# Combining the last three expert tiles on chip instead of two, in a mixture-of-experts kernel

## The chip, the cores and the metric

One core of a Trainium2 chip runs the whole program. The metric is the time of one execution on the device, in microseconds (us). Engines are named as in the profile: PE is TensorE, DVE VectorE, ACT ScalarE, POOL GpSimd, SP SyncE.

## The reference

One transformer-like block over 512 tokens of width 1024, in float32: a gated mixer, then a mixture of experts, then a final norm. Only the end matters here:

```python
x = x + g_f * grouped_moe(hf, ...)      # every token goes to 2 of 16 experts
return rmsnorm(x, final_norm_g)
# grouped_moe, per token t and expert e, combine[t, e] the weight of its two experts, else 0:
g = jnp.einsum('td,edf->tef', t, w_gate)
u = jnp.einsum('td,edf->tef', t, w_up)
a = jax.nn.silu(g) * u * combine[:, :, None]
y = jnp.einsum('tef,efd->td', a, w_down)     # d = 1024, f = 512
```

## The kernel before

The tokens of each expert are gathered into tiles of up to 128 rows. There are 16 tiles and as many more as experts have over 128 tokens; with these inputs the number `tiles` is 17. Each float32 product is made of three passes of `fp32r` on TensorE: a matrix is split into `hi` (a rounded copy, made by ScalarE) and `lo` (the rest, a subtraction on VectorE, L747, that reads both from SBUF), and L1321 to L1323 are hi·hi, hi·lo, lo·hi. Raw weights land in six slots of `raw`, their splits lie in six slots of `wsplit`.

Per tile i, TensorE does `gate_up`, the index of tile i + 2 and the turn of the gathered rows of tile i + 1, then `down` of tile i − 1, and turns the hidden tile (`turn_hidden`, L1575) for the next `down`. VectorE makes one-hot selections, six `lo` splits, `hidden` (L1209: silu(gate) · up), `a_lo` (L1213, the low part of the turned hidden tile `aT`) and `results` (L1227), which scales the tile's output into `y` in SBUF. GpSimd gathers the rows of a tile from DRAM (L461) and scatters `y` into a table of pairs in DRAM (L469): each token has two rows there, one for each expert. Rows that don't belong to a tile have a destination past the table's end and aren't written.

The end of the program, the tail, is written out by hand on every engine:

- The last two tiles are not scattered. Their scaled outputs stay on chip, split into `y_hi`/`y_lo`, and TensorE adds them to the right tokens by one-hot matrices `tail_sel` (L1267; product L1607 in `tail_add(j, t, part, ...)`, j the tile, t the part of 128 tokens, two halves of 512 columns each, into the PSUM pair of t). With 2 tiles, 4 parts, hi and lo and 2 halves there are 32 such products.
- The next-to-last tile's output lies in PSUM banks 5 and 6 (scaling L1277, ScalarE's `y_hi` L714, `y_lo` L1280), the last one's in banks 2 and 3 (L1292, L717, L1298).
- SyncE loads the final norm's gain row (L406), waits for the last scatter (`scattered`) and for all slots of `raw` to be free (`lo_ready`), then reads the table back as four blocks of 1 MB (L410), one for each part of 128 tokens, into slots 2 to 5 of `raw`.
- GpSimd adds the two rows of each pair (L503, one 128x1024 sum for each part, behind `y_in[t]`), VectorE adds that sum to `x_tiles` (L1285, `pair_added(t)`), and later the PSUM pair (L1307). ScalarE squares (L721), VectorE takes the root (L758 to L770) and scales parts 2 and 3 (L1313), GpSimd and ScalarE parts 0 and 1 (L510, L726), and four DMAs write the output.

All buffers are placed by hand, all waits are semaphores with counts; the order on an engine is the order in which its instructions are written.

The two lines that hold SyncE in the tail are

```python
wait_reg(sp, scattered, tiles * 16 - 32)      # 15 scatters of 16 counts each
wait_reg(sp, lo_ready, tiles * 6 + 30)        # all six slots of raw have been split
```

Of the kernel before, what the change touches and what calls it, by code (L numbers as in the profile page):

```python
# [11 lines left out]
ds = bass.ds  # L12
# [30 lines left out]
TILES_MAX = E + 8  # L43
LAST_BANK = 2
SKIP = 2048


def tokens_moe_kernel(nc, A, out):
# [18 lines left out]
    with ctx:  # L67
        def sb(name, shape, dt=F32):
            return ctx.enter_context(nc.sbuf_tensor(name, shape, dt))
# [44 lines left out]
        aT = sb("aT", [P, 2, NF, P], F32R)  # L114
        with nc.sbuf_tensor("below_tail", [P, 3 * D], F32), nc.sbuf_tensor("tail_sel", [P, 2, SEQ], F32R) as tail_sel:
            pass
# [23 lines left out]
        rt = work[:, 3 * D + NT * P:5 * D]  # L140
        gfin = work[:, 4 * D:5 * D]
        y_hi = [wsplit[:, 2 + j, 0, 0:D] for j in range(2)]
        y_lo = [wsplit[:, 2 + j, 1, 0:D] for j in range(2)]
        pair = [ps[:, 0:2, :], ps[:, 4:6, :], ps[:, 6:8, :], ps[:, 2:4, :]]
# [128 lines left out]
        def _(sp):  # L273
# [128 lines left out]
            for c in range(2):  # L402
                wait_reg(sp, lo_ready, tiles * 6 + (25 + c))
                load(c, w_down[ds(e, 1), :, 2 * c:2 * c + 2, :].rearrange("a p k f -> (a p) k f"), 2)

            sp.dma_start(gfin, A["final_norm_g"].partition_broadcast(P)).then_inc(gfin_in, 16)  # L406
            wait_reg(sp, scattered, tiles * 16 - 32)
            wait_reg(sp, lo_ready, tiles * 6 + 30)
            for t in range(NT):
                sp.dma_start(raw[:, t + 2, :], y_pairs[t]).then_inc(y_in[t], 16)  # L410
            for t in range(2, NT):
# [6 lines left out]
        def _(pool):  # L418
# [75 lines left out]
            tiles = pool.value_load(expert_of[0:1, 31:32], min_val=0, max_val=7) + E  # L494
            with pool.Fori(2, tiles - 1) as i:
                gather(i + 2)
                scatter(i - 1)
            wait_reg(pool, gathered, tiles * 16 + 16)
            wait_reg(pool, scattered, tiles * 16 - 32)

# [13 lines left out]
        def _(act):  # L514
# [190 lines left out]
            for c in range(2):  # L705
                act.wait_ge(landed[c], tiles * 16 + 14 * 16)
                act.wait_ge(chunk_used, tiles * 6 + (25 + c))
                A_(wsplit[:, c, 0, :], raw[:, c, :], ACT.Copy).then_inc(hi_ready, 1)
            act.wait_ge(chunk_used, tiles * 6 + 30)
            a_hi(tiles - 1)  # L710

            act.wait_ge(y_ready, tiles - 1)
            act.wait_ge(chunk_used, tiles * 6 + 28)
            A_(y_hi[0].rearrange("p (b n) -> p b n", b=2), ps[:, 5:7, :], ACT.Copy).then_inc(tail_hi, 1)  # L714
            for half in range(2):
                act.wait_ge(y_ready, tiles + half)
                A_(y_hi[1][:, half * 512:half * 512 + 512], ps[:, LAST_BANK + half, :], ACT.Copy).then_inc(tail_hi, 1)  # L717

# [14 lines left out]
        def _(dve):  # L733
# [524 lines left out]
            with dve.Fori(2, tiles - 1) as i:  # L1258
                tile(i, expert_ahead(i), i * 6 + 34, True, i * 6 + 36)
            step(V.tensor_scalar(tail_idx[:, :], row_dest[:, ds(tiles - 2, 2)], 1, None, ALU.logical_shift_right))  # L1260
            done()
            step(V.tensor_copy(tail_tok[:, :], tail_idx[:, :]))
            done()
            dve.wait_ge(idx_mm, tiles + 1)
            for j in range(2):
                for t in range(NT):
                    ins = V.tensor_scalar(tail_sel[:, j, t * P:(t + 1) * P], iota1[:, :], float(t * P - 1),  # L1267
                                          tail_tok[:, j:j + 1], ALU.add, ALU.is_equal)
            ins.then_inc(tail_sel_ready, 1)
            hidden(tiles - 1, tiles * 6 + 28)  # L1270
            for c in range(2):
                dve.wait_ge(hi_ready, tiles * 6 + (31 + c))
                lo(c, c)
            a_lo(tiles - 1)
            dve.wait_ge(chunk_used, tiles * 6 + 30)
            y_53 = ps[:, 5:7, :].rearrange("p b n -> p (b n)")
            V.scalar_tensor_tensor(out=y_53, in0=y_53, scalar=row_w[:, ds(tiles - 2, 1)], in1=gf, op0=ALU.mult,  # L1277
                                   op1=ALU.mult).then_inc(y_ready, 1)
            dve.wait_ge(tail_hi, 1)
            V.tensor_tensor(y_lo[0], y_53, y_hi[0].bitcast(F32), ALU.subtract).then_inc(tail_lo, 1)  # L1280

            def pair_added(t):

                dve.wait_ge(y_sum, t + 1)
                V.tensor_tensor(x_tiles[:, t, :], x_tiles[:, t, :], raw[:, t + 2, 0:D], ALU.add).then_inc(y_added, 1)  # L1285

            pair_added(0)
            pair_added(1)
# [6 lines left out]
            for half in range(2):  # L1295
                c = slice(half * 512, half * 512 + 512)
                dve.wait_ge(tail_hi, half + 2)
                V.tensor_tensor(y_lo[1][:, c], ps[:, LAST_BANK + half, :], y_hi[1][:, c].bitcast(F32),  # L1298
                                ALU.subtract).then_inc(tail_lo, 1)
# [18 lines left out]
        def _(pe):  # L1318
# [280 lines left out]
            with pe.Fori(2, tiles - 1) as i:  # L1599
                tile(i, expert_ahead(i))  # L1600
            gate_up(tiles - 1, tiles * 6 + 24, 0)
            down(tiles - 2, tiles * 6 + 28, between=lambda: turn_hidden(tiles - 1))
            down(tiles - 1, tiles * 6 + 30, 0, LAST_BANK)

            def tail_add(j, t, part, first, last):
# [4 lines left out]
                return mm  # L1610

            pe.wait_ge(tail_sel_ready, 1)
            pe.wait_ge(tail_lo, 1)
            pe.wait_ge(idx_ready, tiles + 1)
            for t in range(NT - 1):
                tail_add(0, t, 0, True, False)
                tail_add(0, t, 1, False, False)
            pe.wait_ge(tail_hi, 3)
            tail_add(1, 0, 0, False, False)
            pe.wait_ge(tail_lo, 3)  # L1620
            tail_add(1, 0, 1, False, True).then_inc(tail_mm, 1)
# [29 lines left out]
```

## Time and profile before

| | |
|---|---|
| median of 3 runs | 811.03 us (810.52 to 811.32) |
| profiled execution, span of its instructions | 808.6 us |
| what lies around the span, by the median | 2.43 us |
| PE busy | 740.2 us (92%) |
| DVE busy | 600.2 us (74%) |
| ACT busy | 383.4 us (47%) |
| POOL busy | 196.5 us (24%) |
| last weight split of the loop ends | 763.4 us |
| last output DMA issued | 803.3 us |

The profiled execution's own time is given as its span, from the first to the last instruction; the median of the runs is the device's time of other executions, and the 2.43 us are the difference of the two. TensorE is busy nearly all the time up to about 783 us; behind that the span holds some 25 us in which sums, norm and output follow each other.

### The profile page before, as it was taken

The page shows a single profiled execution, that of the slowest core. Times are in us where ns is not written, and L with a number is a line of the kernel's source. Part 1 is how long each engine was busy: PE and PEld are TensorE (multiplying, and loading weights), DVE is VectorE, ACT ScalarE, POOL GpSimd, SP SyncE. Part 2 cuts the span into 40 slices and gives each one's busy share as a digit, 9 for nine tenths or more (in the row PEclk, how much of TensorE's full clock was granted, in tenths as well). Part 3 has the DMA queues.
Part 4 walks back from the last instruction along what each step waited for, and adds up shares of the span by engine and source line. Part 5 has one row for each costly group of instructions (what it writes and reads, how often), then busy time and mean ns, then how long its engine had stood idle before and what let it go on. Part 6 is the DMA issues. An engine that isn't in the chain of part 4 may idle for free. (4 is left out here: it accounts for less than half of the span.)

```text
span 808.6 us, 10644 instructions
## 1 busy us (share of the span) xinstructions
PE 740.2 (92%) x3359; PEld 604.0 (75%) x3360; DVE 600.2 (74%) x823; ACT 383.4 (47%) x339; POOL 196.5 (24%) x74
## 2 busy tenths in 40 slices
PE   2589999999999999999999379999999999999982
PEld 2468888866888888887788368888888888888861
DVE  3772334766476666658556789999999999999976
ACT  5533523342323141324133266777777777777613
POOL 1000000400100000000052111445555554444552
PEclk9799999999999999999997589999999999999997
DMA  8797330431356473917472627599999999999652
GB/s 314 258 364 238 104 130 6 151 104 53 106 173 191 159 255 102 313 52 260 159 251 85 199 104 288 214 372 393 369 356 361 361 360 376 366 393 367 248 221 104
DMA packets 105075, 187.66 MB, mean 232 GB/s; under 512 B 6927, under 2 KB 49999, under 8 KB 104540
## 3 DMA queue, kind: packets, MB, share of 16 engines
q1 hardware_dynamic: 98652, 177.77, 61.8%
q0 software_dynamic: 4784, 7.95, 2.7%
q10 hardware_dynamic: 1616, 1.65, 0.6%
q8 instruction: 13, 0.21, 0.1%
q14 instruction: 10, 0.08, 0.0%
HBM read 180.47 MB, written 16.25 MB: 243 GB/s over the span
## 5 line engine op out<-in xcount | busy, mean ns | idle before, releaser
L747 DVE TENSOR_TENSOR wsplit<-raw,wsplit 128x2048 fp32r<-128x2048 f32 x132 | 299.3, 2288 | 78.9 <-ACT wsplit L521 53.8
L684 ACT ACTIVATE wsplit<-raw 128x2048 fp32r<-128x2048 f32 x96 | 183.9, 1918 | 74.3 <-PE ps L1323 74.3
L469 POOL DMA_INDIRECT expert_rows<-work,dest_now x15 | 108.1, 7209 | 114.3 <-DVE work L1227 114.3
L1321 PE MATMUL ps<-wsplit,hgT 128*128 128x512 f32 x272 | 110.1, 405 | 5.0 <-DVE hgT L1146 5.0
L1323 PE MATMUL ps<-wsplit,hgT 128*128 128x512 f32 x272 | 107.6, 395 | 0.0
L1322 PE MATMUL ps<-wsplit,hgT 128*128 128x512 f32 x272 | 106.8, 392 | 0.0
L1321 PE MATMUL ps<-hT,wsplit 128*128 128x512 f32 x256 | 102.5, 400 | 1.0 <-DVE mx L900 1.0
L1322 PE MATMUL ps<-hT,wsplit 128*128 128x512 f32 x256 | 101.1, 395 | 0.0
L1323 PE MATMUL ps<-hT,wsplit 128*128 128x512 f32 x256 | 101.1, 395 | 0.0
L799 DVE SCALAR_TENSOR_TENSOR raw<-raw,c_silu 128x256 f32 (+1 forms) x128 | 62.0, 484 | 17.1 <-DMA raw<-in_w_ada 13.1
L1321 PEld LDWEIGHTS ps<-wsplit,hgT 128*128 128x128 f32 x272 | 51.9, 191 | 15.6 <-DVE hgT L1146 5.7
L1323 PEld LDWEIGHTS ps<-wsplit,hgT 128*128 128x128 f32 x272 | 51.7, 190 | 12.1
L1322 PEld LDWEIGHTS ps<-wsplit,hgT 128*128 128x128 f32 x272 | 52.0, 191 | 10.9
L1321 PE MATMUL ps<-wsplit,hT 128*128 128x512 f32 x128 | 52.2, 408 | 7.7 <-DVE hT L848 6.8
L477 POOL TENSOR_TENSOR wsplit<-raw,wsplit 128x2048 fp32r<-128x2048 f32 x2 | 9.3, 4634 | 203.1 <-ACT wsplit L521 203.0
L1321 PEld LDWEIGHTS ps<-hT,wsplit 128*128 128x128 f32 x256 | 48.1, 188 | 13.5 <-issue 1.9
L521 ACT ACTIVATE wsplit<-raw 128x2048 fp32r<-128x2048 f32 x20 | 38.2, 1916 | 41.2 <-PE ps L1323 15.6
L1322 PEld LDWEIGHTS ps<-hT,wsplit 128*128 128x128 f32 x256 | 48.1, 188 | 12.0 <-issue 0.7
L1323 PEld LDWEIGHTS ps<-hT,wsplit 128*128 128x128 f32 x256 | 48.0, 188 | 11.6
L1321 PE MATMUL ps<-wsplit,aT 128*128 128x512 f32 x136 | 55.1, 405 | 1.5 <-DVE aT L1213 1.5
L628 ACT ACTIVATE wsplit<-raw 128x2048 fp32r<-128x2048 f32 x16 | 30.7, 1917 | 52.1 <-PE ps L1323 33.8
L1323 PE MATMUL ps<-wsplit,aT 128*128 128x512 f32 x136 | 53.4, 392 | 0.0
(241 smaller groups left out, 1207.7 us busy)
## 6 DMA issues: line engine op xcount, KB each, us to landing
raw<-in_w_exp_gate SPq DMA_DIRECT2D x32, 1024.0 KB
raw<-in_w_exp_up SPq DMA_DIRECT2D x32, 1024.0 KB
raw<-in_w_exp_down SPq DMA_DIRECT2D x32, 1024.0 KB
raw<-in_w_ada SPq DMA_DIRECT2D x24, 1024.0 KB
raw<-in_w_in SPq DMA_DIRECT2D x20, 1024.0 KB
expert_rows<-tmp SPq DMA_DIRECT2D x4, 1024.0 KB, 12.4
raw<-in_w_branch_a SPq DMA_DIRECT2D x4, 1024.0 KB
raw<-in_w_branch_b SPq DMA_DIRECT2D x4, 1024.0 KB
```

What stands on the lines that cost most here:

```text
L469: g.indirect_dma_start(out=y_dram, out_offset=bass.IndirectOffsetOnAxis(ap=dest_now[:, 0:1], axis=0), in_=y, in_offset=None, bounds_check= ...
L477: g.tensor_tensor(wsplit[:, c + 2, 1, :], raw[:, c + 2, :], wsplit[:, c + 2, 0, :].bitcast(F32), ALU.subtract).then_inc(lo_ready, 1)
L521: A_(wsplit[:, n, 0, :], raw[:, slot, :], ACT.Copy).then_inc(hi_ready, 1)
L628: A_(wsplit[:, (j + 1) % 2, 0, :], raw[:, (j + 1) % 4, :], ACT.Copy).then_inc(hi_ready, 1)
L684: A_(wsplit[:, c, 0, :], raw[:, c, :], ACT.Copy).then_inc(hi_ready, 1)
L747: V.tensor_tensor(wsplit[:, n, 1, :], raw[:, slot, :], wsplit[:, n, 0, :].bitcast(F32), ALU.subtract).then_inc(lo_ready, 1)
L799: ins = V.scalar_tensor_tensor(out=acc, in0=raw[:, slot, k * CC:(k + 1) * CC], scalar=c_silu[:, k:k + 1], in1=acc, op0=ALU.mult, op1=ALU.add)
L1321: nc.tensor.matmul(out, w_hi, m_hi_, start=first, stop=False)
L1322: nc.tensor.matmul(out, w_hi, m_lo_, start=False, stop=False)
L1323: return nc.tensor.matmul(out, w_lo, m_hi_, start=False, stop=last)
```

## The change

1. The last three tiles, not two, stay on chip. Tile `tiles - 3` goes through `results` in the loop as before, so its scaled output lies in `y` in SBUF. It isn't scattered: the GpSimd loop is one shorter, and its last gather is written out behind it. ScalarE splits `y` into `y_hi[0]` once the last `gate_up` is done, VectorE makes `y_lo[0]` (L1287 in the new file), and `tail_sel` has three one-hot matrices. There are 48 products for 32.
2. On VectorE the tail's order changes: `lo(0)`, then `hidden`, `lo(1)`, `y_lo[0]`, `a_lo`.
3. On TensorE the first four products (tile 0 of the three, part 0) stand between the two last `down`; the others follow the last `down`.
4. SyncE waits for 14 scatters, not 15, and for each read for that slot alone, not for all.
5. The gain row goes to `hg`, the buffer of gathered rows, behind the reads and behind the last gather's landing, since the third one-hot matrix lies where the row was.

```diff
@@ -44,2 +44,3 @@
 LAST_BANK = 2
+TAIL = 3
 SKIP = 2048
@@ -103,4 +104,4 @@
         dest_now = sb("dest_now", [P, 1], I32)
-        tail_idx = sb("tail_idx", [P, 2], I32)
-        tail_tok = sb("tail_tok", [P, 2])
+        tail_idx = sb("tail_idx", [P, TAIL], I32)
+        tail_tok = sb("tail_tok", [P, TAIL])
         signal = sb("signal", [1, RING, E])
@@ -114,3 +115,3 @@
         aT = sb("aT", [P, 2, NF, P], F32R)
-        with nc.sbuf_tensor("below_tail", [P, 3 * D], F32), nc.sbuf_tensor("tail_sel", [P, 2, SEQ], F32R) as tail_sel:
+        with nc.sbuf_tensor("below_tail", [P, 3 * D], F32), nc.sbuf_tensor("tail_sel", [P, TAIL, SEQ], F32R) as tail_sel:
             pass
@@ -140,5 +141,5 @@
         rt = work[:, 3 * D + NT * P:5 * D]
-        gfin = work[:, 4 * D:5 * D]
-        y_hi = [wsplit[:, 2 + j, 0, 0:D] for j in range(2)]
-        y_lo = [wsplit[:, 2 + j, 1, 0:D] for j in range(2)]
+        gfin = hg
+        y_hi = [wsplit[:, 2 + j // 2, 0, j % 2 * D:(j % 2 + 1) * D] for j in range(TAIL)]
+        y_lo = [wsplit[:, 2 + j // 2, 1, j % 2 * D:(j % 2 + 1) * D] for j in range(TAIL)]
         pair = [ps[:, 0:2, :], ps[:, 4:6, :], ps[:, 6:8, :], ps[:, 2:4, :]]
@@ -405,7 +406,8 @@
 
-            sp.dma_start(gfin, A["final_norm_g"].partition_broadcast(P)).then_inc(gfin_in, 16)
-            wait_reg(sp, scattered, tiles * 16 - 32)
-            wait_reg(sp, lo_ready, tiles * 6 + 30)
+            wait_reg(sp, scattered, tiles * 16 - 48)
             for t in range(NT):
+                wait_reg(sp, lo_ready, tiles * 6 + (27 + t))
                 sp.dma_start(raw[:, t + 2, :], y_pairs[t]).then_inc(y_in[t], 16)
+            wait_reg(sp, gathered, tiles * 16 + 16)
+            sp.dma_start(gfin, A["final_norm_g"].partition_broadcast(P)).then_inc(gfin_in, 16)
             for t in range(2, NT):
@@ -494,7 +496,8 @@
             tiles = pool.value_load(expert_of[0:1, 31:32], min_val=0, max_val=7) + E
-            with pool.Fori(2, tiles - 1) as i:
+            with pool.Fori(2, tiles - 2) as i:
                 gather(i + 2)
                 scatter(i - 1)
+            gather(tiles)
             wait_reg(pool, gathered, tiles * 16 + 16)
-            wait_reg(pool, scattered, tiles * 16 - 32)
+            wait_reg(pool, scattered, tiles * 16 - 48)
 
@@ -708,2 +711,5 @@
                 A_(wsplit[:, c, 0, :], raw[:, c, :], ACT.Copy).then_inc(hi_ready, 1)
+            act.wait_ge(y_ready, tiles - 2)
+            act.wait_ge(chunk_used, tiles * 6 + 28)
+            A_(y_hi[0], y, ACT.Copy).then_inc(tail_hi, 1)
             act.wait_ge(chunk_used, tiles * 6 + 30)
@@ -712,7 +718,6 @@
             act.wait_ge(y_ready, tiles - 1)
-            act.wait_ge(chunk_used, tiles * 6 + 28)
-            A_(y_hi[0].rearrange("p (b n) -> p b n", b=2), ps[:, 5:7, :], ACT.Copy).then_inc(tail_hi, 1)
+            A_(y_hi[1].rearrange("p (b n) -> p b n", b=2), ps[:, 5:7, :], ACT.Copy).then_inc(tail_hi, 1)
             for half in range(2):
                 act.wait_ge(y_ready, tiles + half)
-                A_(y_hi[1][:, half * 512:half * 512 + 512], ps[:, LAST_BANK + half, :], ACT.Copy).then_inc(tail_hi, 1)
+                A_(y_hi[2][:, half * 512:half * 512 + 512], ps[:, LAST_BANK + half, :], ACT.Copy).then_inc(tail_hi, 1)
 
@@ -1259,3 +1264,3 @@
                 tile(i, expert_ahead(i), i * 6 + 34, True, i * 6 + 36)
-            step(V.tensor_scalar(tail_idx[:, :], row_dest[:, ds(tiles - 2, 2)], 1, None, ALU.logical_shift_right))
+            step(V.tensor_scalar(tail_idx[:, :], row_dest[:, ds(tiles - 3, TAIL)], 1, None, ALU.logical_shift_right))
             done()
@@ -1264,3 +1269,3 @@
             dve.wait_ge(idx_mm, tiles + 1)
-            for j in range(2):
+            for j in range(TAIL):
                 for t in range(NT):
@@ -1269,13 +1274,2 @@
             ins.then_inc(tail_sel_ready, 1)
-            hidden(tiles - 1, tiles * 6 + 28)
-            for c in range(2):
-                dve.wait_ge(hi_ready, tiles * 6 + (31 + c))
-                lo(c, c)
-            a_lo(tiles - 1)
-            dve.wait_ge(chunk_used, tiles * 6 + 30)
-            y_53 = ps[:, 5:7, :].rearrange("p b n -> p (b n)")
-            V.scalar_tensor_tensor(out=y_53, in0=y_53, scalar=row_w[:, ds(tiles - 2, 1)], in1=gf, op0=ALU.mult,
-                                   op1=ALU.mult).then_inc(y_ready, 1)
-            dve.wait_ge(tail_hi, 1)
-            V.tensor_tensor(y_lo[0], y_53, y_hi[0].bitcast(F32), ALU.subtract).then_inc(tail_lo, 1)
 
@@ -1286,2 +1280,16 @@
 
+            dve.wait_ge(hi_ready, tiles * 6 + 31)
+            lo(0, 0)
+            hidden(tiles - 1, tiles * 6 + 28)
+            dve.wait_ge(hi_ready, tiles * 6 + 32)
+            lo(1, 1)
+            dve.wait_ge(tail_hi, 1)
+            V.tensor_tensor(y_lo[0], y, y_hi[0].bitcast(F32), ALU.subtract).then_inc(tail_lo, 1)
+            a_lo(tiles - 1)
+            dve.wait_ge(chunk_used, tiles * 6 + 30)
+            y_53 = ps[:, 5:7, :].rearrange("p b n -> p (b n)")
+            V.scalar_tensor_tensor(out=y_53, in0=y_53, scalar=row_w[:, ds(tiles - 2, 1)], in1=gf, op0=ALU.mult,
+                                   op1=ALU.mult).then_inc(y_ready, 1)
+            dve.wait_ge(tail_hi, 2)
+            V.tensor_tensor(y_lo[1], y_53, y_hi[1].bitcast(F32), ALU.subtract).then_inc(tail_lo, 1)
             pair_added(0)
@@ -1296,4 +1304,4 @@
                 c = slice(half * 512, half * 512 + 512)
-                dve.wait_ge(tail_hi, half + 2)
-                V.tensor_tensor(y_lo[1][:, c], ps[:, LAST_BANK + half, :], y_hi[1][:, c].bitcast(F32),
+                dve.wait_ge(tail_hi, half + 3)
+                V.tensor_tensor(y_lo[2][:, c], ps[:, LAST_BANK + half, :], y_hi[2][:, c].bitcast(F32),
                                 ALU.subtract).then_inc(tail_lo, 1)
@@ -1600,6 +1608,2 @@
                 tile(i, expert_ahead(i))
-            gate_up(tiles - 1, tiles * 6 + 24, 0)
-            down(tiles - 2, tiles * 6 + 28, between=lambda: turn_hidden(tiles - 1))
-            down(tiles - 1, tiles * 6 + 30, 0, LAST_BANK)
-
             def tail_add(j, t, part, first, last):
@@ -1611,14 +1615,14 @@
 
+            gate_up(tiles - 1, tiles * 6 + 24, 0)
+            down(tiles - 2, tiles * 6 + 28, between=lambda: turn_hidden(tiles - 1))
             pe.wait_ge(tail_sel_ready, 1)
             pe.wait_ge(tail_lo, 1)
+            tail_add(0, 0, 0, True, False)
+            tail_add(0, 0, 1, False, False)
+            down(tiles - 1, tiles * 6 + 30, 0, LAST_BANK)
+
+            pe.wait_ge(tail_lo, 2)
             pe.wait_ge(idx_ready, tiles + 1)
             for t in range(NT - 1):
-                tail_add(0, t, 0, True, False)
-                tail_add(0, t, 1, False, False)
-            pe.wait_ge(tail_hi, 3)
-            tail_add(1, 0, 0, False, False)
-            pe.wait_ge(tail_lo, 3)
-            tail_add(1, 0, 1, False, True).then_inc(tail_mm, 1)
-            for t in range(1, NT):
-                if t == NT - 1:
+                if t:
                     tail_add(0, t, 0, True, False)
@@ -1626,3 +1630,14 @@
                 tail_add(1, t, 0, False, False)
-                tail_add(1, t, 1, False, True).then_inc(tail_mm, 1)
+                tail_add(1, t, 1, False, False)
+            pe.wait_ge(tail_hi, 4)
+            tail_add(2, 0, 0, False, False)
+            pe.wait_ge(tail_lo, 4)
+            tail_add(2, 0, 1, False, True).then_inc(tail_mm, 1)
+            for t in range(1, NT):
+                if t == NT - 1:
+                    for j in range(2):
+                        tail_add(j, t, 0, j == 0, False)
+                        tail_add(j, t, 1, False, False)
+                tail_add(2, t, 0, False, False)
+                tail_add(2, t, 1, False, True).then_inc(tail_mm, 1)
 
```

The tail on VectorE before, from the one-hot matrices to the scaling of the last tile (`wsplit<-ps` is a `y_lo`, `work<-ps` is `hidden`, `mx<-mx,raw` is `pair_added`):

```order
L1267 TENSOR_SCALAR tail_sel<-iota,tail_tok 128x128 [waits idx_mm]
L1267 TENSOR_SCALAR tail_sel<-iota,tail_tok 128x128 x7
...
L1209 TENSOR_TENSOR work<-ps,work 128x512 [waits a_trans]
...
L747 TENSOR_TENSOR wsplit<-raw,wsplit 128x2048 [waits hi_ready]
...
L747 TENSOR_TENSOR wsplit<-raw,wsplit 128x2048 [waits hi_ready]
L1213 TENSOR_TENSOR aT<-ps,aT 128x512 [waits aT_hi]
...
L1277 SCALAR_TENSOR_TENSOR ps<-ps,row_w,tmp 128x1024
L1280 TENSOR_TENSOR wsplit<-ps,wsplit 128x1024 [waits tail_hi]
L1285 TENSOR_TENSOR mx<-mx,raw 128x1024 [waits y_sum] x2
```

The same stretch of the changed kernel (L752 is the split, L1214 `hidden`, L1279 `pair_added`):

```order
L1272 TENSOR_SCALAR tail_sel<-iota,tail_tok 128x128 [waits idx_mm]
L1272 TENSOR_SCALAR tail_sel<-iota,tail_tok 128x128 x11
...
L752 TENSOR_TENSOR wsplit<-raw,wsplit 128x2048 [waits hi_ready]
...
L1214 TENSOR_TENSOR work<-ps,work 128x512 [waits a_trans]
...
L752 TENSOR_TENSOR wsplit<-raw,wsplit 128x2048 [waits hi_ready]
L1287 TENSOR_TENSOR wsplit<-work,wsplit 128x1024 [waits tail_hi]
L1218 TENSOR_TENSOR aT<-ps,aT 128x512 [waits aT_hi]
...
L1291 SCALAR_TENSOR_TENSOR ps<-ps,row_w,tmp 128x1024
L1294 TENSOR_TENSOR wsplit<-ps,wsplit 128x1024 [waits tail_hi]
L1279 TENSOR_TENSOR mx<-mx,raw 128x1024 [waits y_sum] x2
```

One split stands ahead of `hidden`, the split of the tile in `work` (that is `y`) ahead of `aT`, and there are four selections more.

TensorE of the changed kernel, from the last three products of the next-to-last `down` to the first three of the last:

```order
L1329 MATMUL ps<-wsplit,aT 128x512
L1330 MATMUL ps<-wsplit,aT 128x512
L1331 MATMUL ps<-wsplit,aT 128x512
L1611 MATMUL ps<-wsplit,tail_sel 128x512 [waits tail_lo,tail_sel_ready]
L1611 MATMUL ps<-wsplit,tail_sel 128x512 x3
...
L1329 MATMUL ps<-wsplit,aT 128x512 [waits lo_ready]
L1330 MATMUL ps<-wsplit,aT 128x512
L1331 MATMUL ps<-wsplit,aT 128x512
```

The two rows of L1611 are new there; before, the rows of the last `down` with their wait for `aT_lo` followed at once. Behind the last `down` the changed kernel has

```order
L1611 MATMUL ps<-wsplit,tail_sel 128x512 [waits idx_ready]
L1611 MATMUL ps<-wsplit,tail_sel 128x512 x19
L1611 MATMUL ps<-wsplit,tail_sel 128x512 [waits tail_hi]
L1611 MATMUL ps<-wsplit,tail_sel 128x512
L1611 MATMUL ps<-wsplit,tail_sel 128x512 [waits tail_lo]
L1611 MATMUL ps<-wsplit,tail_sel 128x512 x21
```

where before 12 products stood ahead of the wait for `tail_hi`, and 20 from there on.

## Rows read from the trace of the kernel before

**Rows 1.** The page: the span.
```profile
span 808.6 us, 10644 instructions
```

**Rows 2.** The chain that ended last, in order of time: start, length, what.
```profile
783.83 3.23 issue
787.06 1.40 DVE ps L1292 x2
```

**Rows 3.** Timeline of TensorE: start, length, line, tiles, count [idle before].
```profile
773.13 0.60 PE L1575 MATMUL ps<-ident,work 128*128 128x128 f32 x4
...
777.98 0.50 PE L1321 MATMUL ps<-wsplit,aT 128*128 128x512 f32 x1 [1.49 <-DVE aT L1213]
...
783.58 2.92 PE L1607 MATMUL ps<-wsplit,tail_sel 128*128 128x512 f32 x12
789.15 5.13 PE L1607 MATMUL ps<-wsplit,tail_sel 128*128 128x512 f32 x20 [2.65 <-ACT wsplit L717]
```

**Rows 4.** Timeline of VectorE (DVE), the columns of rows 3.
```profile
747.97 6.69 DVE L747 TENSOR_TENSOR wsplit<-raw,wsplit 128x2048 fp32r<-128x2048 f32 x3
...
758.70 4.70 DVE L747 TENSOR_TENSOR wsplit<-raw,wsplit 128x2048 fp32r<-128x2048 f32 x2
...
765.66 1.76 DVE L1267 TENSOR_SCALAR tail_sel<-iota,tail_tok 128x128 fp32r<-128x128 f32 x8
770.66 0.69 DVE L1209 TENSOR_TENSOR work<-ps,work 128x512 f32<-128x512 f32 x1 [3.25 <-PE ps L1323]
771.27 4.48 DVE L747 TENSOR_TENSOR wsplit<-raw,wsplit 128x2048 fp32r<-128x2048 f32 x2
...
777.16 0.69 DVE L1213 TENSOR_TENSOR aT<-ps,aT 128x512 fp32r<-128x512 f32 x1 [1.40 <-ACT aT L677]
777.76 1.28 DVE L1277 SCALAR_TENSOR_TENSOR ps<-ps,row_w,tmp 128x1024 f32<-128x1024 f32 x1
780.22 1.23 DVE L1280 TENSOR_TENSOR wsplit<-ps,wsplit 128x1024 fp32r<-128x1024 f32 x1 [1.17 <-ACT wsplit L714]
781.36 2.42 DVE L1285 TENSOR_TENSOR mx<-mx,raw 128x1024 f32<-128x1024 f32 x1
783.71 3.43 DVE L1285 TENSOR_TENSOR mx<-mx,raw 128x1024 f32<-128x1024 f32 x1
...
789.74 2.35 DVE L1285 TENSOR_TENSOR mx<-mx,raw 128x1024 f32<-128x1024 f32 x2
792.00 4.61 DVE L1307 TENSOR_TENSOR mx<-ps,mx 128x1024 f32<-128x1024 f32 x4
```

**Rows 5.** Timeline of GpSimd (POOL), the columns of rows 3.
```profile
747.88 7.65 POOL L469 DMA_INDIRECT expert_rows<-work,dest_now  x1 [7.57 <-DVE work L1227]
...
766.11 1.01 POOL L469 DMA_INDIRECT expert_rows<-work,dest_now  x1 [7.56 <-DVE work L1227]
774.65 3.33 POOL L503 TENSOR_TENSOR raw<-raw 128x1024 f32<-128x1024 f32 x1 [7.53 <-DMA raw<-expert_rows]
...
780.28 2.42 POOL L503 TENSOR_TENSOR raw<-raw 128x1024 f32<-128x1024 f32 x1
782.65 3.40 POOL L503 TENSOR_TENSOR raw<-raw 128x1024 f32<-128x1024 f32 x1
```

**Rows 6.** The reads of the pair table (L410): SyncE's timeline, then the line's landings.
```profile
769.67 2.00 SPq L410 DMA_DIRECT2D raw<-expert_rows  x4
...
DMA to landing us min/median/max: 4.8/7.9/10.9
```

**Rows 7.** The fourteenth scatter alone (L469, 745 to 760 us).
```profile
DMA to landing us min/median/max: 13.5/13.5/13.5
```

**Rows 8.** The fifteen scatters (L469) of the whole span.
```profile
DMA to landing us min/median/max: 3.3/14.1/15.1
```

**Rows 9.** DMA issues, 640 to 809 us: KB each, us to landing.
```profile
work<-in_final_norm_g SPq DMA_DIRECT2D x1, 512.0 KB, 11.1
```

**Rows 10.** Timeline of ScalarE (ACT), the columns of rows 3.
```profile
776.53 0.60 ACT L677 ACTIVATE aT<-ps 128x512 fp32r<-128x512 f32 x1 [7.16 <-PE ps L1323]
```

More of the change, by code:

```diff
@@ L404, in _ @@
                 load(c, w_down[ds(e, 1), :, 2 * c:2 * c + 2, :].rearrange("a p k f -> (a p) k f"), 2)
+            wait_reg(sp, scattered, tiles * 16 - 48)
+            for t in range(NT):
+                wait_reg(sp, lo_ready, tiles * 6 + (27 + t))
+                sp.dma_start(raw[:, t + 2, :], y_pairs[t]).then_inc(y_in[t], 16)
+            wait_reg(sp, gathered, tiles * 16 + 16)
             sp.dma_start(gfin, A["final_norm_g"].partition_broadcast(P)).then_inc(gfin_in, 16)
-            wait_reg(sp, scattered, tiles * 16 - 32)
-            wait_reg(sp, lo_ready, tiles * 6 + 30)
-            for t in range(NT):
-                sp.dma_start(raw[:, t + 2, :], y_pairs[t]).then_inc(y_in[t], 16)
             for t in range(2, NT):
@@ L1269, in _, with pair_added @@
             ins.then_inc(tail_sel_ready, 1)
+            def pair_added(t):
+                dve.wait_ge(y_sum, t + 1)
+                V.tensor_tensor(x_tiles[:, t, :], x_tiles[:, t, :], raw[:, t + 2, 0:D], ALU.add).then_inc(y_added, 1)
+            dve.wait_ge(hi_ready, tiles * 6 + 31)
+            lo(0, 0)
             hidden(tiles - 1, tiles * 6 + 28)
-            for c in range(2):
-                dve.wait_ge(hi_ready, tiles * 6 + (31 + c))
-                lo(c, c)
+            dve.wait_ge(hi_ready, tiles * 6 + 32)
+            lo(1, 1)
+            dve.wait_ge(tail_hi, 1)
+            V.tensor_tensor(y_lo[0], y, y_hi[0].bitcast(F32), ALU.subtract).then_inc(tail_lo, 1)
             a_lo(tiles - 1)
@@ L1278, in _ @@
                                    op1=ALU.mult).then_inc(y_ready, 1)
-            dve.wait_ge(tail_hi, 1)
-            V.tensor_tensor(y_lo[0], y_53, y_hi[0].bitcast(F32), ALU.subtract).then_inc(tail_lo, 1)
-            def pair_added(t):
-                dve.wait_ge(y_sum, t + 1)
-                V.tensor_tensor(x_tiles[:, t, :], x_tiles[:, t, :], raw[:, t + 2, 0:D], ALU.add).then_inc(y_added, 1)
+            dve.wait_ge(tail_hi, 2)
+            V.tensor_tensor(y_lo[1], y_53, y_hi[1].bitcast(F32), ALU.subtract).then_inc(tail_lo, 1)
             pair_added(0)
```

## The prediction

> **What bounds the kernel now.** I read the page's span and groups first, then the chain of waits over the tail, then the timelines of VectorE, GpSimd and TensorE there, last the landing times of the DMAs. The span is 808.6 us [rows 1]; the runs shown have a median of 811.03 us, 2.43 above the span. My sum is made against the span and its difference is added to the median. The steady part of the kernel is TensorE work that the change doesn't touch, so only what follows 763 us counts.
>
> The chain there runs from the turned hidden tile through `aT`, the scaling and splitting of the next-to-last tile and two sums into `x_tiles` to a stretch of 3.23 us put down to "issue", and at 787.06 to the scaling of the last tile [rows 2]. TensorE had finished that tile's `down` at about 783.7: it starts the one-hot products at 783.58, right behind, and does 12 of them [rows 3]. So VectorE is 3.3 us late, and the reason stands in two timelines [rows 4, 5]: its second sum L1285 takes 3.43 us, where one in peace takes 1.13 (792.00 less 789.74, two of them). It ends at 787.14, 1.1 us behind GpSimd's last pair sum (782.65 + 3.40 = 786.05). That one began as VectorE's first sum still ran. GpSimd's sum alone takes 2.42 us, the one of 3.40 waited for VectorE. They take turns.
>
> So GpSimd's sums, which start when the first read lands (774.65), delay the tail. The reads are issued at 769.67 [rows 6], since they wait for the scatter issued at 766.11 [rows 5], the fifteenth and last.
>
> **The read side of the change.** The fifteenth scatter goes; the fourteenth was issued at 747.88 and landed 13.5 us later [rows 7], at 761.4. With the same 0.27 us from landing to issue as before (the fifteenth landed 3.3 us after 766.11, the shortest of all [rows 8], and the read went at 769.67), the first read goes out at 761.7, 8.0 us earlier. First landing to GpSimd's start took 774.65 − 769.67 = 5.0 us; so sum 0 can start at **766.65**. The second read landed some 2.4 us behind the first and the fourth 7.4 (4.8 to 10.9 us after issues some 1.3 us apart [rows 6]), so the others land near 769.1, 771.5 and 774. The fourth waits for slot 5, whose split ends at 763.4 [rows 4], and comes hardly later. The gain's row moves behind the reads; it took 11.1 us [rows 9], so it lands before 786 and is wanted at 792: no cost.
>
> **The VectorE side.** Per tile of the tail one multiplication (1.28 us as L1227 or L1277) stays; added are 4 selections: the 8 of before span 1.76 us, spacing 0.21, so 12 end at 768.3, in idle time (3.25 us stood before 770.66). Added is one split `y_lo[0]` of 128x1024; the nearest row is L1280, 1.23 us. The order changes too: split lo(0) goes ahead of `hidden`, then lo(1), `y_lo[0]`, and only then `a_lo`. Without GpSimd this fits: lo(0) 768.3 to 770.5, `hidden` 770.66 to 771.3, lo(1) to 773.5, `y_lo[0]` to 774.7, and `a_lo` needs its input at 777.16 only. ScalarE's added copy of 1024 columns (0.60 us for the 512 of L677, so 1.2 at most) falls into the 7.16 us in which ScalarE stood before 776.53 [rows 10], and it is wanted at 773.5.
>
> But GpSimd now sums in that very stretch. A split lo(c) reads two tensors in SBUF, and so does `y_lo[0]`, whose source `y` lies in SBUF, not in PSUM as for the other two tiles. The trace shows what such a pair does [rows 4, 5]: GpSimd's first sum began at 774.65 under the second of two L747 (771.27, 4.48 us) that ran to 775.75 and took 3.33 us instead of 2.42. `a_lo` and L1277, which read PSUM and one SBUF tensor, kept their 0.69 and 1.28 us under GpSimd's sums.
>
> The Trainium skill (SBUF — State Buffer, "Who interferes with whom") says the same in one rule: a VectorE instruction with two SBUF inputs and a GpSimd instruction that reads SBUF exclude each other for the whole instruction. This trace agrees, with 3.43 us for 1.13. By that rule the sum is the 811.7 below; were it not to hold here, it would be the 809.5 of rival 1.
>
> With turns of 2.27 us for GpSimd (783.78 to 786.05) and 2.2 for a split:
> - sum 0 766.65 to 769.05; lo(0) waits, 769.05 to 771.25
> - sum 1 waits, to 773.5; `hidden` 771.25 to 771.9, in time for TensorE's turn at 773.13 [rows 3]
> - lo(1) waits, 773.5 to 775.7; sum 2 waits, to 778.0
> - `y_lo[0]` waits, to 779.1; `a_lo` 779.0 to 779.7 instead of 777.16 to 777.85.
>
> **TensorE.** It now does 4 products of tile 0 ahead of the last `down`, and they wait for `y_lo[0]`. In peace they fit into the 1.49 us gap at 776.5 [rows 3]. Here they start at 779.2 and take 0.32 + 3 × 0.23 us, so `down` starts at 780.2 instead of 777.98: 2.2 us late. `down` takes 783.58 − 777.98 = 5.6, so the products start at 785.8. Before, 32 products stood there, 12 of them in VectorE's shadow; now 48 − 4 = 44, at 0.23 us each (12 in 2.92 us with a last of 0.39): the last starts at 785.8 + 43 × 0.23 = 795.7 and ends at 796.1. The final addition of part 3 follows, 1.2 us: **797.3**. VectorE is ahead: its sums are long ready, the last tile's scaling starts at 786.0, the sums 2 and 3 end at 791. Before, the four additions ended at 792.00 + 4.61 = 796.6 [rows 4]. What is behind (squares, root, scaling, output) is the same. So the end is 0.7 us later: 811.03 + 0.7 = **811.7 us**. 3.3 us of waiting go, and come back as 2.2 us in front of `down` and as a TensorE queue of 16 more products.
>
> Bounds of the unknown: the first sum can start a little earlier, as the gain's transfer is no longer beside the fourteenth scatter (from the end of its issue, 755.53, it took 5.9 us, the fifteenth with nothing beside it 2.3; that is 3.6 at most, but the weight loads stay beside it, so I allow about 1), or later by 0.6 if it lands like the median of the fifteen, 14.1 us [rows 8]. I keep the 761.4 of the row. Up to the turn of rival 2 the end moves by −0.6 to +0.6, so this case's own range is 811.1 to 812.3.
>
> **Rivals.**
> 1. *No turns: VectorE keeps its place* (chance 0.2). For it: a scatter's GpSimd part, alone 1.01 us, took 7.65 under three L747 in a row (747.97, 6.69 us), as if it never got in between them [rows 4, 5]. Against it: VectorE's sum, GpSimd's, VectorE's from 781.36 on, in turns. If lo(1) and `y_lo[0]` run together, `a_lo` is on time, `down` starts at 777.98, the 44 products end at 793.8, the additions at 795.1: 1.5 us earlier, **809.5**. More can't be had, since TensorE's queue then sets the end.
> 2. *Slower: a third turn* (0.25). If the second read lands before VectorE reaches lo(0) at 768.3, sum 1 follows sum 0 at once and lo(0) waits for both, to 772.6; `hidden` ends at 773.2, at the edge of TensorE's turn; lo(1) ends at 777.05 behind sum 2, `y_lo[0]` at 780.4 behind sum 3. `down` starts at 781.5, the end is 2.0 us later: **813.0**. It decides from 0.8 us: the second landing at 769.1 needs to come that much sooner, which the gain's removed transfer could give. A first landing up to 1.6 us later leads to the same place, each part of that delay being added until 768.3 is passed.
> 3. *The change doesn't do what it says* (0.05): the reads go no sooner, because another wait holds them. Then VectorE and GpSimd meet as before, 20 products fit between 783.6 and 789.15, the other 24 end near 795.2, and the additions end at 796.6 as they did: 811.0. The landing at 761.4 and the slots' splits, done by 763.4, speak against it [rows 4, 7].
>
> **How the numbers follow.** Forecast 0.5, rival 1 0.2, rival 2 0.25, rival 3 0.05. About 0.2% (1.62 us) is what a measurement of this kernel can tell from no change. Slower by more: rival 2, and a little of the forecast's upper end, 0.26. Faster by more: rival 1 stands at 1.5 us, just inside; if a row is off by 0.2 us it is out, so 0.12. The same: 0.62. The range 809.4 to 813.3 takes in rivals 1 and 2, and leaves out their far ends.
>
> **What would show it.** Right: reads issued near 761.7; L1272's 12 selections end at 768.3; the split at 768.3 lasts about 3 us and the next about 4, `y_lo[0]` over 3; the gap before the last `down` is about 2.5 us in front of the 4 products; TensorE has no gap from 785.8 to the end of the products; VectorE waits for TensorE before its fourth final addition. Wrong: splits of 2.29 us beside GpSimd's sums, `down` at 778.0 (rival 1), or a turn of the hidden tile later than 773.5 (rival 2), or a gap in TensorE's products.

## The result, and the profile after

The changed kernel takes 819.11 us (median of 6 runs, 818.0 to 821.03) where the kernel before has 811.57 beside it (810.52 to 813.09). The ratio is 1.0099, with a 95% interval of 1.0085 to 1.0112: 7.5 us or 1% slower, far outside the range that was given.

The profile's page has

```profile
span 816.8 us, 10684 instructions
```

8.2 us more than before [rows 1]. The profiled execution was already 0.84 us behind when the loop's last pair of splits began (759.54 against 758.70, the two rows of L752 below and L747 [rows 4]); where I compare places I take these 0.84 us off. The timeline of VectorE in the changed kernel, from the last pair of splits on (L752 is the split, L1272 a selection, L1214 `hidden`, L1315 the final addition; columns as in rows 3):

```profile
759.54 4.69 DVE L752 TENSOR_TENSOR wsplit<-raw,wsplit 128x2048 fp32r<-128x2048 f32 x2
...
766.50 11.26 DVE L1272 TENSOR_SCALAR tail_sel<-iota,tail_tok 128x128 fp32r<-128x128 f32 x12
777.68 2.28 DVE L752 TENSOR_TENSOR wsplit<-raw,wsplit 128x2048 fp32r<-128x2048 f32 x1
779.88 0.68 DVE L1214 TENSOR_TENSOR work<-ps,work 128x512 f32<-128x512 f32 x1
...
803.64 1.23 DVE L1315 TENSOR_TENSOR mx<-ps,mx 128x1024 f32<-128x1024 f32 x1 [1.09 <-PE ps L1611]
```

The 12 selections took 11.26 us, where 8 had taken 1.76 [rows 4]. Everything behind them is late: `hidden` begins at 779.88, not 770.66. Four of the twelve hold nearly all of it. The first and the last of them:

```profile
768.07 2.53 DVE L1272 TENSOR_SCALAR tail_sel<-iota,tail_tok 128x128 fp32r<-128x128 f32 x1
...
775.33 2.43 DVE L1272 TENSOR_SCALAR tail_sel<-iota,tail_tok 128x128 fp32r<-128x128 f32 x1
```

A selection lasts 0.28 us (the median of the twelve). These four lasted 2.43 to 2.53 each. GpSimd's four pair sums stand beside them:

```profile
767.95 9.72 POOL L506 TENSOR_TENSOR raw<-raw 128x1024 f32<-128x1024 f32 x4 [8.57 <-DMA raw<-expert_rows]
```

9.72 us for four, 2.43 each: in peace, as the 2.42 of rows 5. Each of the four selections ends about 0.1 us behind the end of a sum (the first at 770.60, the sum at 770.51). So VectorE made one selection for each sum and stood still otherwise. The chain of waits shows the same, and what followed:

```profile
768.49 2.03 issue
770.52 0.94 DVE tail_sel L1272
771.57 1.37 issue
772.94 4.82 DVE tail_sel L1272 x2
777.76 2.20 DVE wsplit L752
...
781.73 0.43 PE ps L1329
...
785.57 0.23 PE ps L1329
...
787.76 0.49 PE ps L1329
```

Of the stretch to 777.76, 0.94 and 4.82 us are put down to the selections and 2.03 and 1.37 to "issue", in which the engine waited for nothing that the profile names. That is how this wait reads: no semaphore is in it, only instructions far longer than their size. TensorE waited for `hidden` and then ran slowly. Its timeline, then the stretch behind the wait in the changed kernel, and the same stretch in the kernel before (PEclk, the granted clock, follows the busy times):

```profile
780.62 1.12 PE L1583 MATMUL ps<-ident,work 128*128 128x128 f32 x4 [6.49 <-DVE work L1214]
...
787.76 0.49 PE L1329 MATMUL ps<-wsplit,aT 128*128 128x512 f32 x1 [0.57 <-DVE aT L1218]
```

```profile
core 0: us, PE busy (x) PEld busy (x) DVE busy (x) ACT busy (x) POOL busy (x), PEclk, DMA share, GB/s
...
780.00:785.00 5.00, 4.38 (x13) 3.62 (x14) 3.90 (x3) 0.00 (x0) 0.00 (x0) 0.50 0.00 0
```

```profile
780.00:785.00 5.00, 5.00 (x24) 4.09 (x23) 4.78 (x3) 0.19 (x1) 5.00 (x3) 1.00 0.25 100
```

It stood 6.49 us ahead of the hidden tile's turn, and behind that the granted clock was 0.50, the level of 1.2 GHz; the same stretch had 1.00 before. In the chain the products of the half `down` are 0.43 us apart, nine of them from 781.73 on, and 0.23 from 785.57. That is 9 × 0.20 us, and the turn itself took 1.12 us for the 0.60 of [rows 3]: 2.3 us. The last `down` starts at 787.76 where it was 777.98: less 0.84, 8.9 us late.

The reads did what they were to do (SyncE's timeline, and the landing of the fourteenth scatter, L471):

```profile
762.98 2.20 SPq L410 DMA_DIRECT2D raw<-expert_rows  x4
```

```profile
DMA to landing us min/median/max: 13.7/13.7/13.7
```

### The profile page after: what moved, and what is told of

Read it like the earlier page. It is cut to its first block and busy times, and to the rows that moved or that the text cites. A ratio compares the mean times of both kernels' runs of the same rounds, so it can differ in the third digit from the quotient of the medians.

```text
span 816.8 us, 10684 instructions
## 1 busy us (share of the span) xinstructions
PE 746.4 (91%) x3375; PEld 609.5 (75%) x3376; DVE 607.2 (74%) x828; ACT 384.5 (47%) x340; POOL 193.9 (24%) x73
## 5 line engine op out<-in xcount | busy, mean ns | idle before, releaser
L752 DVE TENSOR_TENSOR wsplit<-raw,wsplit 128x2048 fp32r<-128x2048 f32 x132 | 299.2, 2285 | 79.7 <-ACT wsplit L524 54.1
L471 POOL DMA_INDIRECT expert_rows<-work,dest_now x14 | 107.2, 7656 | 106.7 <-DVE work L1232 106.7
```

The costliest lines, as they stand in the source:

```text
L471: g.indirect_dma_start(out=y_dram, out_offset=bass.IndirectOffsetOnAxis(ap=dest_now[:, 0:1], axis=0), in_=y, in_offset=None, bounds_check= ...
```

## The experiments

Each run is compared with the kernel before, run beside it on the same chip. For the first four that kernel had a median of 811.64 us, for the other four 812.0.

**Run 1: the sums wait for the selections.**

```diff
             wait_reg(pool, scattered, tiles * 16 - 48)
+            pool.wait_ge(tail_sel_ready, 1)
```

> The changed kernel, and GpSimd's pair sums wait until the twelve one-hot selections are written. Theory A (the selections and GpSimd's sums exclude each other, each selection waits for a whole sum): the selections end 2.6 us after they start, near 769.1, `hidden` ends near 772, and about 7.5 us of the loss go. What is left is the turn-taking of the two splits and y_lo[0] with the sums, 1.6 us in front of the last down: near the time before, 811 to 812.5. Rival B (the loss is in the third tile's extra work or in the reads, and the slow selections are only a symptom): under 2 us come back, 817 or more.

Measured 810.91 us (12 runs, 809.45 to 812.83), ratio 0.9994 (0.9982 to 1.0006). The whole loss is gone; the time is 0.1 us below the range that was expected. VectorE and GpSimd there:

```profile
765.76 2.45 DVE L1273 TENSOR_SCALAR tail_sel<-iota,tail_tok 128x128 fp32r<-128x128 f32 x12
...
771.38 3.45 DVE L753 TENSOR_TENSOR wsplit<-raw,wsplit 128x2048 fp32r<-128x2048 f32 x1
774.75 3.41 DVE L1288 TENSOR_TENSOR wsplit<-work,wsplit 128x1024 fp32r<-128x1024 f32 x1
```

```profile
768.44 14.35 POOL L507 TENSOR_TENSOR raw<-raw 128x1024 f32<-128x1024 f32 x4 [9.80 <-DVE tail_sel L1273]
```

The selections take 2.45 us. The second split and `y_lo[0]` (L1288) wait 1.2 and 2.2 us for a sum, as was worked out for two-input instructions. The meeting of selections and sums was the cause of the loss, and one wait takes it away.

**Run 2: the selections read PSUM.** ScalarE copies the 128 numbers once to a free PSUM bank; GpSimd isn't held.

```diff
+            act.wait_ge(idx_ready, tiles + 1)
+            A_(ps[:, 7, 128:256], iota1[:, :], ACT.Copy).then_inc(iota_ps, 1)
             silu(tiles - 1, tiles * 6 + 26)
...
-V.tensor_scalar(tail_sel[:, j, t * P:(t + 1) * P], iota1[:, :],
+V.tensor_scalar(tail_sel[:, j, t * P:(t + 1) * P], ps[:, 7, 128:256],
```

> The changed kernel, with the source of the selections copied once to PSUM by ScalarE, so that a selection reads PSUM and not SBUF; GpSimd's sums start as early as in the changed kernel, near 768. Theory A (a one-input VectorE instruction from SBUF excludes GpSimd, one from PSUM does not): the twelve selections take 2.6 to 3.2 us with GpSimd's first sum beside the last ones. Then the course that was forecast: lo(0) waits about 1.3 us for sum 0, lo(1) and y_lo[0] wait a sum each, down starts 2.8 us later than at its earliest, and the time is 811.5 to 813.5. Rival B (any VectorE write of fp32r or any small instruction waits for GpSimd, wherever its input lies): the selections last over 9 us as now, 818 or more.

Measured 812.78 us (12 runs, 810.79 to 814.01), ratio 1.0009 (0.9998 to 1.002). The first sum begins at 768.69, in the middle of the twelve selections, and none of them waits, with the same count, output and scalars as in the changed kernel. That sum takes its 2.42 us:

```profile
L1276 DVE TENSOR_SCALAR tail_sel<-ps,tail_tok x12: 339/340/350, 767.6 to 770.4; 128x128 fp32r<-128x128 f32 x12
```

```profile
767.59 3.19 DVE L1276 TENSOR_SCALAR tail_sel<-ps,tail_tok 128x128 fp32r<-128x128 f32 x12 [0.19 <-DVE tail_tok L1270]
770.70 2.56 DVE L755 TENSOR_TENSOR wsplit<-raw,wsplit 128x2048 fp32r<-128x2048 f32 x1
...
773.79 3.88 DVE L755 TENSOR_TENSOR wsplit<-raw,wsplit 128x2048 fp32r<-128x2048 f32 x1
777.60 3.38 DVE L1291 TENSOR_TENSOR wsplit<-work,wsplit 128x1024 fp32r<-128x1024 f32 x1
...
797.90 1.22 DVE L1319 TENSOR_TENSOR mx<-ps,mx 128x1024 f32<-128x1024 f32 x1 [1.09 <-PE ps L1615]
```

```profile
768.69 14.54 POOL L507 TENSOR_TENSOR raw<-raw 128x1024 f32<-128x1024 f32 x4 [8.30 <-DMA raw<-expert_rows]
```

So a selection doesn't exclude GpSimd as such: it is where its input lies that decides. Whether the read itself or a mode that comes with it holds GpSimd off, the run doesn't tell. The single selection is slower from PSUM, 0.34 us against the 0.28 in peace from SBUF. The Trainium skill (VectorE: DVE Perf Modes, "Mode 2×_2P — use both read ports for one tensor") says that an operation with one tensor input in SBUF can read both halves of it at once, over both read ports, and that PSUM has one port only. The Trainium skill (SBUF — State Buffer, "Who interferes with whom") names `tensor_scalar` among those that then exclude GpSimd. The 0.06 us and the vanished wait agree with that.

What is left is the course that had been forecast in the main: split 2.56 (forecast about 3, and this run's expectation had it wait 1.3 us for sum 0; it waited 0.3, since the selections end later here), split 3.88, `y_lo[0]` 3.38 us. The loop's last pair of splits began at 760.56, 1.86 us behind the kernel before, and the last final addition ends at 797.90 + 1.22 = 799.12; less 1.86 that is 797.3, the number of the forecast. The ratio's 0.7 us are the forecast's 0.7, but its interval runs from −0.2 to 1.6 us: the time alone can't tell the forecast from no change, and the agreement of the places is the better evidence.

**Run 3: TensorE kept busy in the gap.** 26 products into an unused bank ahead of the hidden tile's turn; nothing reads them.

```diff
+            def warm_and_turn():
+                for n in range(26):
+                    nc.tensor.matmul(ps[:, 7, :], aT[:, 0, 0, :], wblock(4, 0, 0, 512), start=True, stop=True)
+                turn_hidden(tiles - 1)
+
+            pe.wait_ge(idx_ready, tiles + 1)
-            down(tiles - 2, tiles * 6 + 28, between=lambda: turn_hidden(tiles - 1))
+            down(tiles - 2, tiles * 6 + 28, between=warm_and_turn)
```

> The changed kernel, with 26 products into an unused PSUM bank in TensorE's gap of 6.5 us ahead of the hidden tile's turn; nothing reads them. Theory A (the idle time let TensorE's clock fall to 0.50, and the 4 turns and 9 of the 12 products behind it cost 0.43 instead of 0.23 us each): the granted clock stays 1.00, the second half of that down takes 2.7 us, not 4.7, and the end is 2.0 to 2.4 us earlier, 816.5 to 817.3. Rival B (these products are slow for another reason, such as operands that GpSimd or a DMA shares): they stay at 0.43 us, and the time does not move.

Measured 815.95 us (4 runs, 815.24 to 816.43), ratio 1.0056 (1.0041 to 1.007). TensorE, then VectorE's `hidden` and the last final addition, then the stretch that had the clock of 0.50:

```profile
773.35 6.11 PE L1619 MATMUL ps<-wsplit,aT 128*128 128x512 f32 x26
779.88 0.66 PE L1583 MATMUL ps<-ident,work 128*128 128x128 f32 x4 [0.41 <-DVE work L1214]
```

```profile
779.15 0.68 DVE L1214 TENSOR_TENSOR work<-ps,work 128x512 f32<-128x512 f32 x1
...
800.67 1.23 DVE L1315 TENSOR_TENSOR mx<-ps,mx 128x1024 f32<-128x1024 f32 x1 [1.09 <-PE ps L1611]
```

```profile
core 0: us, PE busy (x) PEld busy (x) DVE busy (x) ACT busy (x) POOL busy (x), PEclk, DMA share, GB/s
...
780.00:785.00 5.00, 4.67 (x21) 3.33 (x22) 4.19 (x4) 0.60 (x1) 0.00 (x0) 1.00 0.00 0
```

The clock stays 1.00. From the start of `hidden` to the end of the final additions the changed kernel has 804.87 − 779.88 = 25.0 us, this one 801.90 − 779.15 = 22.75: 2.2 us, inside the 2.0 to 2.4 that were expected. The median isn't: 815.95 lies below the 816.5 to 817.3, 3.2 us under the changed kernel's, with four runs here and six there. Up to `hidden` the two profiled executions differ by another 0.25 us (20.34 and 20.09 from the last pair of splits); what the rest is stays open. So about 2.2 of the 7.5 us were the clock, and the other 5.3 are left, by difference, for the wait.

**Run 4: the sums wait for `y_lo[0]`.** `pool.wait_ge(tail_lo, 1)` in the place of run 1's wait.

> The changed kernel, and GpSimd's pair sums wait for y_lo[0], which is the last of the VectorE instructions ahead of a_lo that read two tensors in SBUF. Theory A (all that the change lost came from GpSimd's sums meeting VectorE ahead of the last down): the last down starts as early as in the kernel before, and the sums start near 775.6 and meet VectorE only behind it, as they did before; 810.3 to 811.5. Rival B (the third tile's own work costs time also in peace, 16 more products on the path): the products then end the kernel, over 812.5.

Measured 811.53 us (12 runs, 809.34 to 812.28), ratio 0.9998 (0.9987 to 1.0008). GpSimd, and VectorE's two pair additions and the scaling of the last tile behind them:

```profile
774.48 10.48 POOL L507 TENSOR_TENSOR raw<-raw 128x1024 f32<-128x1024 f32 x4 [16.39 <-DVE wsplit L1288]
```

```profile
780.83 5.21 DVE L1280 TENSOR_TENSOR mx<-mx,raw 128x1024 f32<-128x1024 f32 x2
785.96 1.40 DVE L1301 SCALAR_TENSOR_TENSOR ps<-ps,row_w,tmp 128x512 f32<-128x512 f32 x2
```

`down` is on time, and the two engines meet behind it, as in the kernel before: 5.21 us for two additions of 1.14. Without the meeting ahead of `down` the third tile costs nothing that these runs can tell, and gives nothing.

**Run 5: run 4, and VectorE adds part 1 later.**

```diff
             pair_added(0)
-            pair_added(1)
             dve.wait_ge(chunk_used, tiles * 6 + 32)
...
+            pair_added(1)
             pair_added(2)
             pair_added(3)
```

> As the run whose sums wait for y_lo[0], and VectorE adds the pair sum of part 1 only behind the last tile's low parts, so that the last tile's scaling doesn't wait for GpSimd's fourth sum. Theory A (VectorE waits there 2.5 us behind GpSimd, and TensorE's 44 products are the floor): scaling starts as the last down ends, the products run without a gap, the fourth final addition waits for TensorE; 0.7 to 0.9 us faster than that run, 810.4 to 811.0 where the kernel before has 811.6. Rival B (VectorE's total work is the bound in either order): no change.

Measured 810.41 us (11 runs, 808.78 to 810.99), ratio 0.9978 (0.9969 to 0.9987). VectorE waits 0.75 us for the last `down` ahead of the scaling and 0.40 for the products ahead of the fourth final addition, and the 44 products have no gap (VectorE, then TensorE):

```profile
786.10 1.42 DVE L1300 SCALAR_TENSOR_TENSOR ps<-ps,row_w,tmp 128x512 f32<-128x512 f32 x2 [0.75 <-PE ps L1332]
...
796.07 1.22 DVE L1316 TENSOR_TENSOR mx<-ps,mx 128x1024 f32<-128x1024 f32 x1 [0.40 <-PE ps L1612]
```

```profile
785.79 10.24 PE L1612 MATMUL ps<-wsplit,tail_sel 128*128 128x512 f32 x44
```

This is TensorE's floor for three tiles in this order. Expected were 0.6 to 1.2 us less than the kernel before; found are about 1.8 by the ratio (1.1 to 2.5).

**Run 6: the kernel before, with that reordering alone.**

> The kernel before, with only that reordering: pair_added(1) behind the last tile's low parts. Theory A (the 3.2 us that VectorE stands behind GpSimd's last sum are the only loss of the tail before, and need neither a third tile nor earlier reads): the last tile's scaling starts near 783.9 instead of 787.06, VectorE then works through to 794.6 without a wait, 2.0 us faster, 809.3 to 809.9 where the kernel before has 811.6. Rival B (the wait only moves, since the same sums and additions are still to be made): within 0.5 us of the kernel before.

Measured 809.82 us (11 runs, 806.98 to 812.19), ratio 0.9974 (0.9962 to 0.9987), about 2.1 us.

```profile
782.81 2.42 DVE L1285 TENSOR_TENSOR mx<-mx,raw 128x1024 f32<-128x1024 f32 x1
785.33 1.42 DVE L1291 SCALAR_TENSOR_TENSOR ps<-ps,row_w,tmp 128x512 f32<-128x512 f32 x2
...
791.42 4.61 DVE L1307 TENSOR_TENSOR mx<-ps,mx 128x1024 f32<-128x1024 f32 x4
```

The additions of part 0 took their turn with a sum (2.42 us), the scaling follows the last `down`, and from there on VectorE has no wait up to the end of the final additions. Two tiles, the reads where they were and one addition moved do as well as three tiles with two repairs.

**Run 7: the kernel before, with parts 0 and 1 both later.**

> The kernel before, with pair_added(0) and pair_added(1) both behind the last tile's low parts. Theory A: GpSimd then makes its four sums without meeting VectorE, and ends near 784.2 instead of 786.1; scaling starts near 783.9; but VectorE has one addition of 1.14 us more behind it, which it could have made in an idle stretch. So 1.0 us faster than the kernel before and 1.0 slower than the run with one moved. Rival B: as that run or better, because no turn is waited for.

Measured 810.99 us (12 runs, 809.55 to 812.82), ratio 0.999 (0.9978 to 1.0001).

```profile
786.57 1.42 DVE L1290 SCALAR_TENSOR_TENSOR ps<-ps,row_w,tmp 128x512 f32<-128x512 f32 x2 [2.43 <-PE ps L1323]
...
789.26 4.62 DVE L1285 TENSOR_TENSOR mx<-mx,raw 128x1024 f32<-128x1024 f32 x4
```

```profile
777.36 10.40 POOL L503 TENSOR_TENSOR raw<-raw 128x1024 f32<-128x1024 f32 x4 [7.56 <-DMA raw<-expert_rows]
```

No addition meets a sum any more (the first sum, 3.30 us, meets the second split as it did before), but VectorE stands 2.43 us idle ahead of the scaling and has the addition to make behind it. It is 0.8 us faster than the kernel before by the ratio, with an interval that just takes in no change, and 1.2 us slower than run 6. Avoiding every meeting isn't the aim: a meeting in an idle stretch is free.

**Run 8: the changed kernel, with the sums in halves.**

```diff
+                for half in range(2):
+                    c = slice(half * 512, half * 512 + 512)
-                g.tensor_tensor(raw[:, t + 2, 0:D], raw[:, t + 2, 0:D], raw[:, t + 2, D:2 * D],
-                                ALU.add).then_inc(y_sum, 1)
+                    ins = g.tensor_tensor(raw[:, t + 2, c], raw[:, t + 2, c],
+                                          raw[:, t + 2, D + half * 512:D + half * 512 + 512], ALU.add)
+                ins.then_inc(y_sum, 1)
```

> The changed kernel, with each of GpSimd's pair sums made in two halves of 512 columns; the first starts as early as now, near 768. Theory A (turns: one selection gets in between two GpSimd instructions, and waits as long as the one it meets): the four selections that are left then wait 1.25 us each instead of 2.4, so the selections end near 773 and not 777.7, then lo(0), lo(1) and y_lo[0] wait a half each; the last down starts near 783.4, not 787.8; the time is 4 to 4.5 us shorter, 814.3 to 815.3. Rival B (VectorE is locked out for as long as GpSimd has work, whatever its pieces): the selections end with the last half, near 778, and the time stays 818 or more.

Measured 815.32 us (10 runs, 811.41 to 818.58), ratio 1.0035 (1.0019 to 1.005). A selection's duration (ns, min/median/max), then all twelve in the timeline with the first split and `hidden` behind them, and the sums:

```profile
L1275 DVE TENSOR_SCALAR tail_sel<-iota,tail_tok x12: 280/1300/1342, 766.8 to 775.2; 128x128 fp32r<-128x128 f32 x12
```

```profile
766.75 9.78 DVE L1275 TENSOR_SCALAR tail_sel<-iota,tail_tok 128x128 fp32r<-128x128 f32 x12
776.46 3.36 DVE L755 TENSOR_TENSOR wsplit<-raw,wsplit 128x2048 fp32r<-128x2048 f32 x1
779.74 0.68 DVE L1217 TENSOR_TENSOR work<-ps,work 128x512 f32<-128x512 f32 x1
```

```profile
767.63 10.04 POOL L508 TENSOR_TENSOR raw<-raw 128x512 f32<-128x512 f32 x8 [7.97 <-DMA raw<-expert_rows]
```

A selection now waits 1.30 us, the length of the half sum that it meets: turns, one for one, and no lockout for as long as there are sums. The selections end at 776.5, though, and not near 773; the median is at the upper edge of the 814.3 to 815.3 that were expected. What I had wrong is the number left over. This profiled execution was the slowest of the ten (818.58). In it the first sum began 0.88 us after the first selection (1.45 in the changed kernel), so seven waited, not four, and the first split waited for the eighth half: `hidden` begins 19.9 us behind the last pair of splits (759.82), where the changed kernel has 20.3. This execution gained next to nothing by the halves; its time, 818.58, is that of the changed kernel's profiled one (818.6). With halves every selection that is still to come costs over 1 us, and how many there are hangs on tenths of a us in the reads' landing. That may be why these times scatter over 7 us, where those of the changed kernel scatter over 3; no other execution was profiled, so it isn't shown. With whole sums the block is as long as all four sums, whether four or ten selections are left.

## Why the prediction was wrong, point by point

- **The step that failed** is "added are 4 selections: the 8 of before span 1.76 us, spacing 0.21, so 12 end at 768.3, in idle time". The duration is right (2.45 us in run 1), the cover isn't there. The forecast put turns only on instructions with two tensors in SBUF, since those were the ones that the trace of before showed beside a sum. The selections, which read one, never stood beside a sum there. The only GpSimd work beside them was the last scatter's 1.01 us (766.11 [rows 5], selections from 765.66 [rows 4]), and they took no longer for it. So their price beside a sum was unknown and should have been bounded: at 0.21 us below, at one sum of 2.42 us each above. With sum 0 forecast at 766.65 and selections to 768.3, the two overlapped in the forecast's own table. Their meeting makes the split 777.68 − 768.3, less the 0.84 of this execution, so 8.5 us late. Some of that comes back, since the four sums are then over and no later instruction waits for one; the clock adds to it. The end is 804.87 − 0.84 = 804.0 for the 797.3 of the sum, 6.7 us late.
- The Trainium skill (SBUF — State Buffer, "Who interferes with whom") names `tensor_scalar` among the operations that can take both ports and so exclude GpSimd. I used that section's rule for two inputs and not this other one. It would have given a rival with the time of four sums, 9.7 us, ahead of `hidden`.
- **The second loss** had no term at all: that a TensorE idle for 6.5 us comes back at half clock. Run 3 puts 2.2 us on it. The gaps of 1.49 and 2.65 us in the kernel before [rows 3] had left its granted clock at 1.00, so those rows gave no price for a longer one.
- **Reads.** Issue forecast at 761.7, found at 762.98 − 0.84 = 762.1; the scatter landed 13.7 us after its issue for 13.5. Sum 0 forecast at 766.65, found 767.1. Right, within 0.5 us.
- **Turns of the two-input instructions.** Right where the selections don't interfere: run 2 ends at 797.3 on the forecast's own time axis, and its second split of 3.88 us and `y_lo[0]` of 3.38 are those of the list. The first took 2.56 us for about 3. That the end agrees to a tenth is in part luck: the selections from PSUM ended later, and the split behind them waited less.
- **TensorE's queue.** 44 products without a gap, 10.09 us in the changed kernel against 10.3 in the sum, and VectorE waits for it at the fourth addition (1.09 us of idle time). Right, and run 5 shows it as the floor.
- **Rival 1** (VectorE keeps its place between two instructions) fell: wherever GpSimd's sums met VectorE in these runs, the two took turns one for one. The row that spoke for it, a scatter's 7.65 us beside three splits, isn't explained by any run, and the 1.01 us that it was held against weren't taken alone but beside the selections. Its price as the best case, 1.5 us, is near what run 5 gained, about 1.8, since both end by TensorE's queue.
- **Rival 2** was slower by a third turn; the loss had another origin, and in run 2 the first split waited for one sum and not for two. **Rival 3** didn't happen.
- The 3.3 us of VectorE behind GpSimd's last sum were read rightly in the profile before. That they could be had by moving one addition (run 6) was not seen.

## What to carry to other kernels

When a change moves an engine's work in time, list every instruction on the other engine that it will then lie beside, and price each pair from a row where such a pair met; where no row shows it, a bound from above is one partner's length for each instruction, as long as partners are left, and that is ruinous for short ones. Small VectorE instructions from SBUF beside long GpSimd sums were the worst pairing here: one went through for each sum. Before moving more work on chip, look whether the stretch that waits needs only its order changed.

## What the runs showed of the hardware that was not expected

- A 128x128 `tensor_scalar` from SBUF, 0.28 us alone, took 2.4 to 2.5 us beside GpSimd sums of 2.4, and 1.30 beside half sums; the same from PSUM took 0.34 us and didn't wait at all.
- After 6.49 us idle TensorE worked at a granted clock of 0.50 for about 5 us (from 780.6 to 785.6); fed with products whose result nobody reads, it stayed at 1.00. In run 8's profile it stood 6.10 us and came back at 0.50 as well.
